# Branch ends multiplied by token tile, and the memory attention's queries and output taken in halves

## What is computed

```python
for l in range(DEPTH):                      # 2 layers
    xn = rms_norm(h, mix_pre_g[l])
    proj = jnp.einsum('bsd,dc->bsc', xn, w_in[l])
    ...
    h = h + rms_norm(jnp.einsum('bsc,cd->bsd', mix, w_out[l]), mix_post_g[l])
    xa = memory_attention(rms_norm(h, x_pre_g[l]), rms_norm(mem, mem_g[l]), x_wq[l], x_wkv[l], x_wo[l])
    h = h + rms_norm(xa, x_post_g[l])
    ff = swiglu(rms_norm(h, f_pre_g[l]), f_w_gu[l], f_w_down[l])
    h = h + rms_norm(ff, f_post_g[l])
...
h = rms_norm_2(x, norm_w); proj = h @ w_in  # the second block starts so

def memory_attention(h, mem_n, wq, wkv, wo):
    q = jnp.einsum('bsd,dhe->bshe', h, wq)
    ...
    p = jax.nn.softmax(logits, axis=-1)
    o = jnp.einsum('bhsm,bmhe->bshe', p.astype(v.dtype), v)
    return jnp.einsum('bshe,hed->bsd', o, wo)
```

## Time and profile before

| | us |
|---|---|
| median of three runs | 3060.29 |
| the profiled execution | 3060.33 |
| its span in the profile | 3058.5 |
| TensorE busy | 3038.3 |
| VectorE busy | 1979.4 |
| ScalarE busy | 1522.8 |
| from the last product's end to the next product's start, six branch ends | 35.14 |
| from `xq`'s end to `xo0`'s start, each layer | 15.2 |

### The profile page before, as it was taken

The page is one execution under the profiler, slowest core; times in us unless marked ns, Lnnn a source line. Parts: engine busy times, 40 slices in busy tenths (PEclk is TensorE's granted clock), DMA queues, the critical chain, the costliest instruction groups (busy, mean ns, idle before and its releaser), DMA issues.

```text
span 3058.5 us, 44954 instructions
## 1 busy us (share of the span) xinstructions
PE 3038.3 (99%) x16358; PEld 2596.0 (85%) x16358; DVE 1979.4 (65%) x2308; ACT 1522.8 (50%) x1989; POOL 69.1 (2%) x122
## 2 busy tenths in 40 slices
PE   9999999999999999999999999999999999999999
PEld 9998888888888888899888888888888899788887
DVE  6667756555555555767756665655665667888664
ACT  6645546444444444645546455555554555444543
POOL 0000100000000000000100000000000010000000
PEclk9999999999999999999999999999999999999999
DMA  8754554655555555554554666666665555676555
GB/s 331 244 177 159 187 177 143 224 190 192 190 186 193 189 191 180 181 177 160 180 182 140 227 218 203 204 199 207 218 206 194 185 181 182 219 231 223 170 191 173
DMA packets 167933, 596.91 MB, mean 195 GB/s; under 512 B 18845, under 2 KB 26201, under 8 KB 164953
## 3 DMA queue, kind: packets, MB, share of 16 engines
q1 hardware_dynamic: 150432, 545.33, 54.2%
q10 hardware_dynamic: 14888, 36.86, 3.5%
q0 software_dynamic: 2464, 12.67, 1.3%
HBM read 577.99 MB, written 17.07 MB: 195 GB/s over the span
## 4 chain that ended last, share of the span: by engine, by line
PE 91%; DVE 4%; ACT 2%; DVEq 1%; issue 1%; DMA 0%; POOL 0%; POOLq 0%; ACTq 0%; SPq 0%
PE acc L709 24%; PE acc L711 24%; PE acc L710 24%; PE acc L717 5%; PE acc L720 4%; PE acc L719 4%; PE tp L773 1%; DVE lo L1866 1%; ACT hi L1225 1%; PE tp L813 0%; PE tp L936 0%; PE tp L1167 0%; PE acc L762 0%; PE acc L760 0%; PE acc L761 0%
## 5 line engine op out<-in xcount | busy, mean ns | idle before, releaser
L1866 DVE TENSOR_TENSOR lo<-raw,hi 128x1024 fp32r<-128x1024 f32 x1032 | 1244.9, 1214 | 817.3 <-ACT hi L1225 807.0
L1225 ACT ACTIVATE hi<-raw 128x1024 fp32r<-128x1024 f32 x1032 | 1078.4, 1050 | 1185.9 <-PE acc L711 966.2
L709 PE MATMUL acc<-hi,xh 128*128 128x512 f32 (+2 forms) x2504 | 971.3, 388 | 1.8 <-DVE xl L1981 1.2
L711 PE MATMUL acc<-hi,xl 128*128 128x512 f32 (+2 forms) x2504 | 963.6, 385 | 0.0
L710 PE MATMUL acc<-lo,xh 128*128 128x512 f32 (+2 forms) x2504 | 963.0, 385 | 0.0
L709 PEld LDWEIGHTS acc<-hi,xh 128*128 128x128 f32 x2504 | 470.3, 188 | 97.7 <-DVE xl L1981 3.4
L711 PEld LDWEIGHTS acc<-hi,xl 128*128 128x128 f32 x2504 | 470.2, 188 | 93.8
L710 PEld LDWEIGHTS acc<-lo,xh 128*128 128x128 f32 x2504 | 470.6, 188 | 90.1
L717 PE MATMUL acc<-xh,hi 128*128 128x256 f32 x1144 | 329.3, 288 | 1.4 <-ACT qbT L1234 0.5
L719 PE MATMUL acc<-xl,hi 128*128 128x256 f32 x1144 | 323.6, 283 | 0.0
L720 PE MATMUL acc<-xh,lo 128*128 128x256 f32 x1144 | 323.5, 283 | 0.0
(11 more groups left out here) (424 smaller groups left out, 2569.0 us busy)
## 6 DMA issues: line engine op xcount, KB each, us to landing
raw<-in_stream SPq DMA_DIRECT2D x1032, 512.0 KB, 4.2
turn_scratch<-made ACTq DMA_DIRECT2D x8, 1024.0 KB, 6.7
gpost<-in_post_g POOLq DMA_DIRECT2D x6, 1024.0 KB, 5.1
rotc<-turn_scratch ACTq DMA_DIRECT2D x8, 512.0 KB, 5.9
rots<-turn_scratch ACTq DMA_DIRECT2D x8, 512.0 KB, 8.8
u_stack<-u_scratch ACTq DMA_DIRECT2D x24, 128.0 KB, 4.7
h<-in_mem ACTq DMA_DIRECT2D x2, 1024.0 KB, 8.0
xT<-in_x_cols ACTq DMA_DIRECT2D x4, 512.0 KB, 7.1
```

Source lines behind the costliest of these rows:

```text
L709: nc.tensor.matmul(o, ah, high, start=first, stop=False)
L711: last = nc.tensor.matmul(o, al, high, start=False, stop=final)
L1225: nc.scalar.activation(hi[s][:, :, 0:w], raw[s][:, :, 0:w], ACT.Copy).then_inc(hi_done, 1)
L1866: nc.vector.tensor_tensor(lo[s][:, :, 0:w], raw[s][:, :, 0:w], hi[s][:, :, 0:w].bitcast(F32), ALU.subtract).then_inc(split_done, 1)
```

## The change

At each branch end TensorE no longer waits for both token tiles of h. It turns quads 0 and 1 of token tile 0, and multiplies the first four chunks of the next product for token tile 0; then it turns token tile 1 and multiplies the same four chunks for it (`raw_start`). For form C that makes matmuls over 128 tokens where there were matmuls over 256, twice as many. ScalarE and VectorE write `xh` and `xl` of these chunks in pieces of 128x128, tile by tile; VectorE adds token tile 1 to h between the two, its first 512 columns in two pieces. From chunk 4 on the product runs as before, but quad 2 is turned ahead of chunk 7 and quad 3 ahead of chunk 11. VectorE splits units 3 and 4 around h's quad 2, unit 5 behind h's quad 3, and units 6 and 7 behind `xl` of quad 3. The group of unused matmuls ahead of the next product goes, another becomes shorter. In the memory attention ScalarE and VectorE copy half of the queries each, the logits start with the first half, and `xo0` is multiplied token tile by token tile (`tile_product`), the five unused matmuls ahead of it left out.

```diff
--- before.py
+++ after.py
+            def tile_product(pos, g, a_h, a_l, tile_ready):
+
+                pe.wait_ge(acc_read[g.parity], pos.n("acc", g.turn + 1))
+                for t in range(NT):
+                    tile_ready(t)
+                    for n in range(g.units):
+                        s = (g.unit + n) % SLOTS
+                        if t == 0:
+                            pe.wait_ge(split_done, pos.n("unit", g.unit + n + 1 + SLOTS))
+                        for k in range(KU):
+                            c = n * KU + k
+                            o = acc[g.parity][:, t, :]
+                            ah, al = a_h[:, c, t * P:(t + 1) * P], a_l[:, c, t * P:(t + 1) * P]
+                            nc.tensor.matmul(o, ah, hi[s][:, k, :], start=c == 0, stop=False)
+                            nc.tensor.matmul(o, ah, lo[s][:, k, :], start=False, stop=False)
+                            last = nc.tensor.matmul(o, al, hi[s][:, k, :], start=False, stop=c == g.kchunks - 1)
+                        if t == NT - 1:
+                            last.then_inc(unit_used, 1)
...
-            FILL_IN = {0: (6, 3, 4), 1: (1, 4, 4), 2: (3, 3, 4)}
-
-            def raw_norm(pos, k, tag, turns, g):
+            FILL_IN = {0: (6, 2), 1: (1, 2), 2: (3, 2)}
...
+                def chunk(c, t):
+                    s, k_ = (g.unit + c // KU) % SLOTS, c % KU
+                    pe.wait_ge(tile_low, pos.n(24, 8 * k - 8 + 4 * t + c + 1))
...
+                    for b in range(g.blocks):
+                        o = a[:, b, part]
+                        wh, wl = hi[s][:, k_, b * P:(b + 1) * P], lo[s][:, k_, b * P:(b + 1) * P]
+                        nc.tensor.matmul(o, wh, ah, start=c == 0 and t == 0 and b % 2 == 0, stop=False,
+                                         skip_group_check=True)
+                        nc.tensor.matmul(o, wl, ah, start=False, stop=False, skip_group_check=True)
+                        last = nc.tensor.matmul(o, wh, al, start=False, stop=False, skip_group_check=True)
+                    return last
...
+                stay_warm(g.parity, src, before)
+                pe.wait_ge(h_quads, pos.n(24, 8 * k + 1))
+                tile(first, 0, 0).then_inc(tp_early, 1)
+                pe.wait_ge(h_quads, pos.n(24, 8 * k + 2))
+                tile(second, 1, 0)
+                stay_warm(g.parity, src, between)
+                for c in range(4):
+                    if c % KU == 0:
+                        pe.wait_ge(split_done, pos.n("unit", g.unit + c // KU + 1 + SLOTS))
+                    if c == 3:
+                        pe.wait_ge(tile_low, pos.n(24, 8 * k - 8 + 4))
+                        pe.wait_ge(h_first, pos.n(3, k))
+                        tile(first, 0, 1, (0, 1)).then_inc(tp_early, 1)
+                        pe.wait_ge(h_quads, pos.n(24, 8 * k + 3))
+                        tile(first, 0, 1, (2, 3)).then_inc(tp_full, 1)
+                    chunk(c, 0)
+                pe.wait_ge(h_quads, pos.n(24, 8 * k + 4))
+                tile(second, 1, 1).then_inc(tp_full, 1)
+                for c in range(4):
+                    last = chunk(c, 1)
+                    if c % KU == KU - 1:
+                        last.then_inc(unit_used, 1)
+
+                def chunk_ready(c):
+                    q = c // 4
+                    if c % 4 == 0:
                         pe.wait_ge(x_half, pos.n(12, 4 * k + q + 1))
-                    else:
+                    elif c % 4 == 2:
                         after_turn(pe, pos, turns[f"{tag}{q}"])
-                        if q < 2:
-                            quad(q + 2)
-
-                return unit_ready
+                    elif c % 4 == 3 and q < 3:
+                        quad(q + 1)
...
+                o = tp[turns[f"{tag}0"] % 2]
+                for t in range(NT):
+                    part = slice(t * P, (t + 1) * P)
+                    act.wait_ge(tp_early, pos.n(6, 2 * k - 1 + t))
+                    for c in range(4):
+                        if t == 1 and c == 2:
+                            see_turn(act, pos, turns[f"{tag}0"])
+                        nc.scalar.activation(xh[:, c, part], o[:, c, part], ACT.Copy, scale=gain(c)).then_inc(tile_high, 1)
+                    if t == 0:
+                        units.before(pos, g, 0, g.end)
+                for q in range(1, 4):
+                    units.before(pos, g, 2 * q - 2, g.end)
...
-                copy_group(pos, LG["xq"], qxT[:, :, :])
-                act.drain()
+                units.ahead(pos, LG["xq"])
+                a = see_group(act, pos, LG["xq"])
+                nc.scalar.activation(qxT[:, 0:2, :], a[:, 0:2, :], ACT.Copy).then_inc(q_first, 1)
+                act.wait_ge(q_second, pos.n(1, 1))
+                act.drain().then_inc(acc_read[LG["xq"].parity], 1)
...
+                for c in range(4):
+                    if c == 2:
+                        units.before(pos, g, -2, g.end)
+                    low(c, 0).then_inc(tile_low, 1)
+                dve.drain()
+                dve.wait_ge(out_roots, pos.n(6, 2 * k))
+                for n in range(2):
+                    cols = slice(n * W // 2, (n + 1) * W // 2)
+                    nc.vector.scalar_tensor_tensor(h[:, 1, cols], y[:, 1, cols], prs[:, 1:2], h[:, 1, cols],
+                                                   ALU.mult, ALU.add).then_inc((h_first, h_quads)[n], 1)
+                nc.vector.scalar_tensor_tensor(h[:, 1, W:2 * W], y[:, 1, W:2 * W], prs[:, 1:2], h[:, 1, W:2 * W],
+                                               ALU.mult, ALU.add).then_inc(h_quads, 1)
+                for c in range(4):
+                    low(c, 1).then_inc(tile_low, 1)
+                dve.drain().then_inc(tp_read[turns[f"{tag}0"] % 2], 1)
+                dve.sem_inc(x_half, 1)
+                units.before(pos, g, -1, g.end)
+                for q in range(1, 4):
                     o = tp[turns[f"{tag}{q}"] % 2]
                     for c in range(4):
                         if c % 2 == 0:
-                            dve.wait_ge(x_pair, pos.n(24, 8 * k + 2 * q + c // 2 + 1))
+                            dve.wait_ge(x_pair, pos.n(18, 6 * k) + 2 * q + c // 2 + 1)
                         last = nc.vector.scalar_tensor_tensor(xl[:, 4 * q + c, :], o[:, c, :], gain(4 * q + c),
                                                               xh[:, 4 * q + c, :].bitcast(F32), ALU.mult, ALU.subtract)
                         if c == 1:
                             last.then_inc(x_half, 1)
                     last.then_inc(tp_read[turns[f"{tag}{q}"] % 2], 1)
-                    if q < 2:
-                        add_quad(q + 2, add)
-                    units.before(pos, g, 2 * q, g.end)
+                    units.before(pos, g, q - 1 if q < 3 else 2 * q, g.end)
+                    if q == 1 and add:
+                        late = y[:, :, 2 * W:3 * W]
+                        nc.vector.tensor_tensor(late, late, gains(2), ALU.mult)
+                    if q < 3:
+                        add_quad(q + 1, add)
+                        units.before(pos, g, q, g.end)
...
+                a = see_group(dve, pos, LG["xq"])
+                nc.vector.tensor_copy(qxT[:, 2:4, :], a[:, 2:4, :]).then_inc(q_second, 1)
```

More of the change, by code:

```diff
@@ L686, in _, with product @@
         def _(pe):
-            def product(pos, g, a_h, a_l, only=None, quad_ready=None, unit_ready=None, also_read=None):
+            def product(pos, g, a_h, a_l, only=None, quad_ready=None, unit_ready=None, also_read=None,
+                        chunk_ready=None, begin=0):
                 a = (accC if g.form == "C" else acc)[g.parity]
-                for n in range(g.units) if only is None else (only,):
+                for n in range(begin, g.units) if only is None else (only,):
                     if n == 0:
@@ L802, in stay_warm, with raw_start, tile @@
                     nc.tensor.matmul(acc[into][:, 0, :], src[:, 0, 0:P], src[:, 0:2, :], start=True, stop=True)
-            FILL_IN = {0: (6, 3, 4), 1: (1, 4, 4), 2: (3, 3, 4)}
-            def raw_norm(pos, k, tag, turns, g):
+            FILL_IN = {0: (6, 2), 1: (1, 2), 2: (3, 2)}
+            def raw_start(pos, k, tag, turns, g):
                 src = cqh if k else h2h
-                before, between, behind = FILL_IN[k]
-                def tile(o, q, t):
-                    for c in range(4):
+                before, between = FILL_IN[k]
+                a = (accC if g.form == "C" else acc)[g.parity]
+                def tile(o, q, t, chunks=range(4)):
+                    for c in chunks:
                         last = nc.tensor.transpose(o[:, c, t * P:(t + 1) * P],
@@ L909, in _ @@
                             after_turn(pe, pos, LTP["bkv"])
-                        if g.kchunks == KD:
-                            product(pos, g, xh, xl, only=n, unit_ready=ready if g is LG["cq"] else None)
+                        if g is LG["cq"]:
+                            if layer == 0 or n >= 4 // KU:
```

(24 more changed lines are left out.)

70 lines of the change are left out of this document (35 added, 35 removed).

## The result

The changed kernel takes 3087.53 us, median of six runs (3086.46 to 3088.63); the kernel before 3060.23 (3059.44 to 3061.14). The ratio is 1.0089, with a 95% interval of 1.0080 to 1.0099: slower by 27.3 us, inside the predicted 3070 to 3101, and 8.5 above the predicted 3079. The profiled execution took 3086.46.

What follows compares the result with a forecast made beforehand. TensorE, busy 3038.3 of 3058.5 us, was taken as the bound. The terms 2 x 2.2 + 2 x 3.1 + 2 x 6.1 - 2 x 1.9 = +19.0 on 3060.33 gave 3079 us, range 3070 to 3101.

Steps and rivals of the forecast that it cites:

- gate0, both: Two branch ends at `gate0`: 4.1 us lost in waits, 1.9 gained at the start, so +2.2 us each.
- cq and q0, up to the next end: Ends like `gate0` with two more multiplies of 1.22 us on VectorE: +3.1 us each.
- xq, both: Two form C ends: 96 matmuls over 128 tokens at 0.109 us, and waits behind them, +6.1 us each.
- attention, both: Memory attention, twice: 1.6 us gained at `xo0` by token tile, 0.3 by the split query copy, -1.9 each.
- The head: Start of the product at `gate0`: chunk 0 near 507.6 instead of 510.50, chunk 4 2.7 us earlier, 1.9 gained.
- The waits: TensorE at `gate0` waits 0.7 us at chunk 8, 0.7 at chunk 10, 2.7 at chunk 12, for `xl` or `lo`.
- 0.066: Rival at `xq`: short 128-column matmuls step by 0.066 us, if only streaming counts; kernel at 3071 us; chance 0.06.
- 0.218: Rival at `xq`: short matmuls cost 0.218 us each, as full f32 does; kernel at 3100 us; chance 0.20.
- 81 ns: The skill's step for loads and matmuls over 128 columns, applied to `xq`: kernel 5.4 us lower, at 3074; no chance given.
- The clock: Rival: TensorE's clock falls at the waits of six ends, 2.8 us lost each; kernel at 3096 us; chance 0.12.
- a clock row without a fall: Sign expected in the profile after; a slow stretch behind the chunk 12 waits would show the forecast wrong.
- The quads are in time: Rival: behind the first chunks, transposes and splits come without waits, -7.4 us in all; kernel at 3053 us; chance 0.05.

Runs made afterwards that it cites:

- e10_xo0: Kernel before, with `xo0` multiplied token tile by token tile and the five unused matmuls ahead of it dropped, queries still copied by ScalarE alone: 3057.49 us.
- e4_attention: Kernel before, with the change's attention part alone (queries copied half each, `xo0` by token tile, six unused matmuls less): 3056.64 us.
- e5_intime: Changed kernel, with transposes of quads 2 (not at `cq`, `q0`) and 3 one chunk earlier, low parts of units 5 and 6 ahead of those quads' `xl`: 3063.59 us.

## Why the prediction was right, point by point

With the four falls of the clock set aside (4 x 1.7 = 6.8), the terms held (measured on the profiled executions, whose spans differ by 26.2; the medians differ by 27.3):

| | predicted | measured |
|---|---|---|
| gate0, both | +4.4 | 3.9 + 4.0 - 3.4 = +4.5 |
| cq and q0, up to the next end | +6.2 | 5.6 + 4.2 - 3.4 = +6.4 |
| xq, both | +12.2 | 6.25 + 6.25 = +12.5 |
| attention, both | -3.8 | -1.6 - 2.0 = -3.6 |
| start of the kernel | 0 | -0.4 |
| half clock | 0 | 4 x 1.7 = +6.8 |
| sum | +19.0 | +26.2 |

- **The head.** Chunk 0 was foreseen 2.9 us earlier at `gate0` and was 2.83 earlier; chunk 4 2.7 against 2.5.
- **The waits.** 0.7, 0.7 and 2.7 at `gate0` were 0.54, 0.15 to 0.19 and 2.38. They were summed 1.0 too high; small steps that I had not counted, such as 0.46 instead of 0.23 from 518.21 to 518.67 where the chunks of one tile end, made up for most of it. So the agreement of the sum is better than that of its parts. The releaser at chunk 12 is `lo`, as said.
- **`cq` and `q0`.** Chunk 10 of `cq` was foreseen to wait 1.9 and waited 1.46. The +6.4 is in part luck. By the distances of the table above the two ends are 5.3 us longer each, +7.2 without the falls; `q0`'s 4.2 is the whole stretch to the kernel's end, which differs by 1 us between traces in which nothing was changed there.
- **`xq`.** The row of line 1051 was the right neighbour: 0.111 against the 0.109 taken. The two other prices, 0.066 and 0.218, are out. The slope that I took from the weight loads, 0.83 ns for each column, was misread: the earlier trace rows give (192 - 109)/96 = 0.86, which makes 111 ns for 128 columns, the step that was measured. That the load sets the step is still only argued; no run changed one without the other. Here too the parts are off and the sum is not: the waits at chunks 8, 10 and 12 were 0.51, none and 2.33, where 0.6, 0.5 and 2.6 were foreseen, and small steps that I had not counted made up for it.
  The 81 ns of the Trainium skill (TensorE: Matmul & The Clock Gate, section Back-to-back issue gap), which would have given 3074, do not hold for these matmuls: the trace has 0.111.
- **The attention.** 1.6 and 0.3 were 1.7 and 0.4 by e10_xo0 and e4_attention. In the changed kernel one layer gave 1.6 in all: VectorE came to its half of the queries at 474.81, behind a late `lo`, which was the bound named.
- **The clock: the step that failed.** I held a fall for a separate case with a chance of 0.12 and asked for "a clock row without a fall". It fell, on top of the forecast, and with the falls at nothing the sum is 6.8 too low. By my own rule the forecast was wrong in this. Its size was wrong too: I had 2.8 for each from the kernel's opening, a stretch of 5.9 us, and a stretch here is 3.41 and costs 1.7. By six such falls the rival would have stood at 3089, and it would have been the nearest of all.
- **"The quads are in time"** I gave 0.05 and said that VectorE would have to be twice as quick. For the changed kernel as written that held. But it is the order and not the speed that decides it: VectorE idles for 3.50 us ahead of those `xl`, and e5_intime used that time.

## What to carry to other kernels

When work is begun earlier by finer pieces, follow the pieces behind it to the end of the stage: here 2.5 us won at the head were lost by chunk 12, since the next transposes now had six matmuls of cover where they had had 36, and the low part of unit 6 stood behind them on VectorE. Where an engine is late, look at its idle time just ahead of the late work; if there is some, the order may be at fault, and changing it can be one line. A gain on the busiest engine ends where a helper's queue (here ScalarE's squares and the splits behind them) has not moved with it.
